# Routing and expert setup joined into one stage of a hybrid mixer, cross attention and MoE layer

## What is computed

```python
def hier_moe(xn, w_rg, b_rg, w_re, b_re, w_gate, w_up, w_down):
    glog = (xn @ w_rg + b_rg).astype(F32)
    gsel = jnp.argmax(glog, axis=-1)                  # the best of 4 groups
    pg = jnp.take_along_axis(jax.nn.softmax(glog, axis=-1), gsel[:, None], axis=-1)
    elog = (xn @ w_re + b_re).astype(F32).reshape(T, MOE_GROUPS, EXPERTS_PER_GROUP)
    elog = jnp.take_along_axis(elog, gsel[:, None, None], axis=1)[:, 0]
    top_p, top_i = lax.top_k(jax.nn.softmax(elog, axis=-1), TOP_K_INNER)
    gate = pg * top_p / jnp.sum(top_p, axis=-1, keepdims=True)
    ...
    padded = (counts + MOE_BLOCK - 1) // MOE_BLOCK * MOE_BLOCK   # blocks of 128 rows
    ...
    def expert_block(args):
        xb, e = args
        h = jax.nn.silu(xb @ w_gate[e]) * (xb @ w_up[e])
        return h @ w_down[e]
```

## Time and profile before

| | us |
|---|---|
| median of 3 runs | 2595.21 |
| these runs | 2592.27 to 2596.45 |
| the profiled execution | 2593.17 |
| its span, first to last instruction | 2591.3 |
| TensorE busy | 2309.0 (89%) |
| VectorE busy | 1400.4 (54%) |
| ScalarE busy | 981.1 (38%) |
| mean granted TensorE clock | 0.951 of full speed |

### The profile page before, as it was taken

One profiled execution on the slowest core, in us unless ns is written; L12 is line 12 of the kernel. 1 busy time (PEld: TensorE's weight loads), 2 busy tenths in 40 slices (PEclk: granted clock), 3 DMA queues, 4 the chain that ended last, 5 costly groups with the idle time before them and its releaser, 6 DMA issues. The chain is left out here.

```text
span 2591.3 us, 34611 instructions
## 1 busy us (share of the span) xinstructions
PE 2309.0 (89%) x12015; PEld 1308.7 (51%) x12016; DVE 1400.4 (54%) x2029; ACT 981.1 (38%) x1421; POOL 339.3 (13%) x277
## 2 busy tenths in 40 slices
PE   4999999999919988999999998179999999999980
PEld 2465565655618973555555554134444444444440
DVE  5566555664628843333333332757557677757823
ACT  4522533323211332222212221146446577657723
POOL 0022121220220000000000000002221222122212
PEclk8999999999959999999999999589999999999995
DMA  5201001010060133110111001369779999999927
GB/s 187 86 25 58 1 25 58 1 49 1 9 221 25 50 123 124 49 65 34 65 66 60 31 33 49 129 239 346 253 250 302 308 321 342 338 317 328 341 66 283
DMA packets 151797, 366.52 MB, mean 141 GB/s; under 512 B 24720, under 2 KB 30736, under 8 KB 151440
## 3 DMA queue, kind: packets, MB, share of 16 engines
q1 hardware_dynamic: 133120, 305.28, 32.3%
q0 software_dynamic: 13824, 50.34, 8.0%
q10 hardware_dynamic: 4752, 9.51, 1.0%
HBM read 303.75 MB, written 61.34 MB: 141 GB/s over the span
## 5 line engine op out<-in xcount | busy, mean ns | idle before, releaser
L110 PE MATMUL bankA<-wi,hnT 128*128 128x512 f16 (+1 forms) x1536 | 303.3, 356 | 5.5 <-DVE wi L498 5.5
L110 PE MATMUL bankE<-wg,xT 128*128 128x512 f16 x1152 | 262.2, 385 | 25.7 <-DVE xT L2432 21.5
L110 PE MATMUL bankE<-wu,xT 128*128 128x512 f16 x1152 | 259.0, 382 | 0.0
L110 PE MATMUL bankE<-wd,hT 128*128 128x512 f16 x1152 | 256.5, 379 | 1.7 <-DVE hT L2437 1.7
L110 PEld LDWEIGHTS bankA<-wi,hnT 128*128 128x128 f16 x1536 | 151.7, 99 | 148.8 <-issue 7.4
L110 PEld LDWEIGHTS bankE<-wg,xT 128*128 128x128 f16 x1152 | 113.9, 99 | 166.1 <-issue 34.3
L110 PEld LDWEIGHTS bankE<-wd,hT 128*128 128x128 f16 x1152 | 112.6, 98 | 137.6 <-issue 1.9
L110 PE MATMUL bankA<-hnT,wi 128*128 128x512 f16 x768 | 172.3, 387 | 9.0 <-DVE hnT L474 9.0
L110 PEld LDWEIGHTS bankE<-wu,xT 128*128 128x128 f16 x1152 | 113.3, 98 | 127.4 <-issue 3.3
L110 PE MATMUL bankC<-w_probs,probsT 128*128 128x512 f16 x768 | 172.0, 381 | 0.0
L110 PE MATMUL bankC<-score_w,hnT_c 128*128 128x512 f16 x768 | 170.7, 379 | 0.0
(11 more groups left out here) (400 smaller groups left out, 3402.1 us busy)
## 6 DMA issues: line engine op xcount, KB each, us to landing
w_rows<-in_w_gate SPq DMA_DIRECT2D x64, 1024.0 KB
w_rows<-in_w_up SPq DMA_DIRECT2D x64, 1024.0 KB
w_rows<-in_w_down SPq DMA_DIRECT2D x64, 1024.0 KB
xg<-in_x SPq DMA_DIRECT2D x4, 2048.0 KB, 10.9
cat_t<-scratch_cat SPq DMA_DIRECT2D x16, 512.0 KB, 4.9
Hc<-in_x SPq DMA_DIRECT2D x16, 512.0 KB, 5.6
scratch_ybuf<-Hc SPq DMA_DIRECT2D x16, 512.0 KB, 2.6
hf<-scratch_ybuf SPq DMA_DIRECT2D x16, 512.0 KB, 11.8
```

Source lines behind the costliest of these rows:

```text
L110: ins = pe.matmul(o, a[x][k], b[y][k], start=start and k == 0 and j == 0, stop=stop and k == n - 1 and j == 2)
```

## The change

`route` is no longer a stage of its own. Its code stands at the head of each engine's code in `experts`, in the same block. Six things differ:

- the table of constants, now `cst_all` with 784 columns, is loaded once, as the first DMA of the cross stage in the place of the identity alone (128 columns), and kept; the loads of `cst_r`, `iota_e`, `tok_e` and `cst_e` are gone;
- SP loads all six pieces of expert 0 as the first thing of the stage, without reading a plan. So that expert 0 is the first in use in any case, its number of blocks is raised to at least 1 (one more operation on `nblk`);
- VectorE makes the places (`destf`) and the row lists right behind `end`, and the block plan after `rows_to`. A new semaphore `planned` tells it; the engines wait on it before they read `plan` (SP after the first six loads, GpSimd after two gathers, the others at the loop or, for VectorE, in order);
- the gate lists (split of the gates, three multiplications, 32 products) move behind the up products of block 0 on TensorE and behind the rests of gate and up on VectorE; `gate_of` is taken after the rests of down;
- in VectorE's `first`, the rest of x of block 0 moves between the rests of gate and those of up; on ScalarE the nearest values of down come before x;
- the intermediate tiles of the routing lie in slot 1 of `wd` and in `y0` and `y1`, which are free by then, and the products in `bankE`.

The core of the diff:

```diff
-        ident, nhalf, gf = sb("cst_c", [P, P]), sb("nhalf_c", [P, 2]), sb("g_ffn", [P, D])
+        ident, nhalf, gf = cst[:, K_ID:K_ID + P], sb("nhalf_c", [P, 2]), sb("g_ffn", [P, D])
...
-            sp.dma_start(ident[:, :], dram["cst"][:, K_ID:K_ID + P]).then_inc(ld, 16)
+            sp.dma_start(cst[:, :], dram["cst"][:, 0:K_GAM]).then_inc(ld, 16)
...
-            sp.dma_start(iota[:, :], dram["cst"][:, K_IOTA:K_IOTA + P]).then_inc(ld, 16)
-            sp.dma_start(tok[:, :], dram["cst"][:, K_TOK:K_TOK + NCH]).then_inc(ld, 16)
-            sp.dma_start(ident[:, :], dram["cst"][:, K_ID:K_ID + P]).then_inc(ld, 16)
-            e0 = expert(0)
-            for p in GU:
-                load(p, e0)
-            for i in range(HB):
-                sp.wait_ge(x_ld[i], 16)
-            for p in DN:
-                load(p, e0)
+            for p in GU + DN:
+                load(p, slice(0, 1))
+            sp.wait_ge(planned, 1)
             gate_up_rows(1)
...
             LATE = 2
-            for t in range(NT + LATE):
+            gather(0)
+            gather(1)
+            pool.wait_ge(planned, 1)
+            used = turns_used(pool)
+            for t in range(1, NT + LATE):
...
         def steps(eng, first, step, last):
 
+            first()
+            eng.wait_ge(planned, 1)
             used = turns_used(eng)
-            first()
...
             def first():
-                for p in GU:
+                for p in GU + DN:
                     nearest(p, 0, 0)
                 take_x(0, 0)
-                for p in DN:
-                    nearest(p, 0, 0)
                 silu(0, 0)
...
+            do(ts, nblk[:, 0:1], nblk[:, 0:1], 1.0, None, ALU.max)
+            do(dve.tensor_tensor_scan, end[:, :], one, nblk[:, :], 0.0, ALU.mult, ALU.add)
+
+            do(tt, first_blk[:, :], end[:, :], nblk[:, :], ALU.subtract)
+            do(ts, first_row[:, :], first_blk[:, :], float(P), None, ALU.mult)
...
             dve.tensor_scalar(rows_from[:, :], row_f[:, :], float(T - 1), None, ALU.min).then_inc(rows_ok, 1)
             dve.tensor_copy(rows_to[:, :], row_f[:, :]).then_inc(rows_ok, 1)
...
+            do(ts, used_e[:, :], nblk[:, :], 0.0, None, ALU.is_gt)
+            do(dve.tensor_tensor_scan, rank[:, :], one, used_e[:, :], 0.0, ALU.mult, ALU.add)
...
+            dve.wait_ge(cnt, 2)
+            dve.tensor_copy(plan[:, 0:PL_TURNS], bank[6][0:1, 2 * NE:2 * NE + PL_TURNS]).then_inc(planned, 1)
...
             def first():
-                gate_up_rest(0, 0)
+                for p in GU[0:2]:
+                    rest(p, 0, 0)
                 x_rest(0, 0)
+                for p in GU[2:]:
+                    rest(p, 0, 0)
+                gates_listed()
                 down_rest(0, 0)
+                gates_taken()
                 product(0, 0)
...
             def first():
                 turn_x(0, 0, 0)
                 gate_up(0, 0)(0, 0)
+                gates_listed()
                 turn_x(1, 1, 0)
```

More of the change, by code:

```diff
@@ L2141, in experts @@
-def experts(nc, env, dram, gates, destf, plan):
+def experts(nc, env, dram, logits, cst):
     FT = DE // P
@@ new lines, in work @@
+        def work(k, *shape):
+            n = int(np.prod(shape))
+            v = spare[k][:, spent[k]:spent[k] + n]
+            spent[k] += n
+            letters = "abc"[:len(shape)]
+            return v.rearrange(f"p ({' '.join(letters)}) -> p {' '.join(letters)}", **dict(zip(letters, shape)))
+        oh = work(1, 2, NCH, NE)
+        e32, pos = work(2, NCH, NGR, EPG), work(2, NCH, NE)
+        both, before, cum, again = (work(0, NE, NCH) for n in range(4))
+        E8, t8, m8, O8 = (work(0, NCH, EPG) for n in range(4))
@@ new lines, in experts, with flat @@
+        G4, O4, t4 = (work(0, NCH, NGR) for n in range(3))
+        c1 = work(0, 8, NCH)
+        nblk, first_blk, end, used_e, rank, eq, t32, first_row = (work(0, NE) for n in range(8))
+        cols, turns_f = work(0, 6), work(0, 1)
+        c_expert, c_u, c_block, c_split, c_more, c_half = (cols[:, i:i + 1] for i in range(6))
+        lt, ones, one = cst[:, K_LT:K_LT + P], cst[:, K_ONE:K_ONE + P], cst[:, K_ONE:K_ONE + NE]
+        def flat(t):
+            return t[:, :, :].rearrange("p e c -> p (e c)")
@@ L2167, in experts @@
+        row_f, pad_f, gate_of = work(0, NB), work(0, NB), sb("gate_of", [P, NB])
         bank = [ctx.enter_context(nc.psum_tensor(f"bankE{i}", [P, 512], F32)) for i in range(8)]
-        ld = sem("e_consts")
+        r_steps, a_s, cnt, summed, ready, planned = (sem(n) for n in (
+            "route_steps", "route_exp", "counts_done", "pairs_summed", "again_ready", "plan_ready"))
         w_ld = [sem(f"w_rows_loaded{p}") for p in range(6)]
@@ L2368, in _ @@
         def _(dve):
-            dve.wait_ge(ld, 48)
-            ch = Chain(dve, lists)
+            ch = Chain(dve, r_steps)
+            tt, ts, stt, red = dve.tensor_tensor, dve.tensor_scalar, dve.scalar_tensor_tensor, dve.tensor_reduce
+            seen = []
+            dve.memset(again[:, :, :], 1.0).then_inc(ready, 1)
+            dve.wait_ge(ready, 1)
+            dve.memset(again[:, :, 0:1], 0.0).then_inc(ready, 1)
+            dve.wait_ge(ready, 2)
             def do(f, *a):
```

317 lines of the change are left out of this document (135 added, 182 removed).

## The result

| | before | after |
|---|---|---|
| median of 4 runs each, us | 2593.82 | 2575.45 |
| these runs | 2592.27 to 2596.45 | 2574.24 to 2577.27 |
| the profiled execution | 2593.17 | 2574.76 |
| its span | 2591.3 | 2572.9 |

What follows compares the result with a forecast made beforehand. Loop bound by TensorE, its start by a chain mostly on VectorE; gains of 11.74 us up to `rows_to` and 6.67 from there to block 1 sum to 18.4, so 2593.17 becomes 2574.8 us, range 2570 to 2583.

Steps and rivals of the forecast that it cites:

- What bounds: Loop at TensorE's pace, so the kernel's end follows block 1's start, set by a chain mostly on VectorE, 1621 to 1714 us.
- Part 1: Stage start to the end of `rows_to`: 11.74 us shorter, ending at 1655.00 instead of 1666.74.
- The table's 2.31: Stage start: with the table already loaded, VectorE's first reduction comes at 1621.36 instead of 1623.67, saving 2.31 us.
- 3.67 for the change of stage and three constants: Routing on VectorE: the 3.67 us that `blk` sat idle for `cst_e` goes.
- Part 2: From `rows_to` to block 1's gate products: 40.42 us instead of 47.09, a gain of 6.67.
- the rests of down with the gate lists beside them: Ahead of block 1: 4.48 us on VectorE beside 4.44 of lists on TensorE, 4.6 with a semaphore.
- The cover of x: Block 0: gather lands in 6.3 us, x ready at 1664.3 against gate rests ending at 1664.9, 0.6 us spare.
- Rival 1: x or the start-up costs more, together 4 to 7 us, about 2580.5 us; chance 0.14.
- The rule against it: First gather's descriptors beside the plan's short VectorE operations: if GpSimd were kept out, x 2.2 us later, kernel 2576.4.
- The plan's move: Block plan moved behind `rows_to`: 5.52 us leaves part 1 and comes back in part 2.
- The early weights: Expert 0's six pieces, issued at 1620.5, are split at about 1643, 17 us before the first rest.
- The cross stage: Its first DMA grows from 64 to 392 KB: no cost, 1 us if the 2.6 us cover failed.

Runs made afterwards that it cites:

- the last experiment: Three gate multiplications moved from VectorE to GpSimd, against the changed kernel with block 1's x taken before the second expert's up rests: 2569.2 us, 0.9902 of before.
- a third kernel: Gate lists moved back ahead of the first rests on VectorE and TensorE, against the changed kernel: 2583.26 us, 0.9955 of before.

## Why the prediction was right

**What bounds.** The loop passes on what comes ahead of it: shown by 828.7 to 834.3 us for it in all kernels, whether block 1 starts at 69 or at 95 us.

**Part 1** was to give 11.74; it gave 11.39. The table's 2.31 is exact in after, and block 1 moved by 2.56 when it was put back alone. 3.67 for the change of stage and three constants is borne out by the missing gap; it wasn't tested alone. Most of the 0.35 us missing came from a step that the sum didn't have: the count products of the routing, for which VectorE's wait ahead of `nblk` grew from 2.01 to 2.43 us. TensorE made them in 3.80 us at a granted clock of 0.58 in before and in 4.32 at 0.50 in after.

**Part 2** was to give 6.67; it took 39.90 us instead of 40.42. Each of its terms lies within 0.2 us of the rows. The largest two misses: the plan took 5.34 to the first rest instead of 5.52, and for the rests of down with the gate lists beside them I took 4.6, with the lists at 4.44; this step took 4.41. The lists were 2.81, since TensorE came to them at full clock, and lay wholly under the rests of down. The text beside the sum says that `sg` waited for 12.5 us; that is how long block 0's products took, while VectorE was idle for 8.31 of it. The sum doesn't use the figure.

**The cover of x** was given as 0.6 us and was 2.3: ScalarE was done with x at 1661.39 and VectorE came to it at 1663.66. The step that failed is the landing, taken as 6.3 from the earlier trace rows: it was 4.5. Rival 1, x late, lost its ground with that. The gather had been measured beside other work; in its new place it had none.

**The rule against it** had the sign wrong. I had set the plan's short operations beside the multiplications as the same danger. (The prediction's 1658.3 us is where the descriptors would end at 3.00 us, not the issue, which the sum has at 1655.3; a gather kept out until 1660.5 would have been 5.2 us late and not 2.2.) In after the first gather's descriptors took 1.24 and the second's 0.94 us beside the plan's short steps, against 3.00 and 1.74 beside the multiplications. With VectorE idle they took 1.24 and 0.95 too, so the short steps cost nothing that can be seen. The Trainium skill, SBUF — State Buffer, section "Who interferes with whom", says that a VectorE instruction with two SBUF inputs contends with a GpSimd instruction that reads SBUF; the last experiment agrees, with 7.91 and 10.11 us for pairs of rests of 4.47 beside GpSimd's multiplications. The same section infers of `tensor_tensor` that it doesn't hold up the building of descriptors. The runs speak against that: 3.00 us beside the `tensor_tensor` multiplications and 3.00 beside the rests, both with two SBUF inputs, 1.24 without either, and 7.87 for a gather beside four rests in a row (the kernel with x taken later), which ended 0.82 us after the last of them. Whether it is the writing of descriptors that waits, or GpSimd's reading of the row numbers, isn't told apart.

**The plan's move** I booked as −5.52 and +5.52, nothing on the chain but an earlier gather. The sum came out, but the place is worth 7.2 us: 5.4 of earlier issue and 4.6 of shorter landing, less the cover. VectorE takes x in two halves, and the second, which sets the end, had 2.9 us of cover in after: 7.1. What was missing in my account is that each step moved also decides what runs beside the others.

**The early weights.** That they were ready I had; that the new order of ScalarE rests on them I hadn't seen, and the first kernel without them showed it by 8.5 us.

**The cross stage** was to cost nothing: the cat tile is turned 9.34 us after the stage's first DMA, 9.37 before, with 328 KB more ahead of it. Its landing took 6.8 us instead of 5.9, inside the cover.

**What the parts are worth**, each undone alone, in us of block 1's start: weights early 11.1 (19.6 with ScalarE's order), gate lists later 8.7, plan behind the lists 7.2, table 2.6. They sum to 29.6, more than the 18.6 measured, so such prices don't add: each was taken from a kernel that is arranged for all the others. The early weights show it. In before the four pieces of gate and up were split by 1669.85, 10 us ahead of VectorE's first rest (1679.90); there, early weights alone had nothing to shorten. That is read from the rows; no kernel had them alone.

## What to carry to other kernels

Put short work that nobody waits for yet (here the block plan) right behind the step that starts a transfer, and the long operations behind the landing; price a transfer by what will run beside it in its new place, not by its old row. Where an engine waits at the head of a loop, list what the waiting instruction really needs, and move all else on the supplying engine behind it: a few lines of order gave a further 5.8 us here. And before work is given to an idle engine, look at what that engine shares with the one to be relieved.

## What the runs showed of the hardware

- The first indirect gather of 128 rows landed in 4.5 to 4.7 us beside short steps of VectorE or none, 6.2 beside VectorE's rests, 9.1 beside the rests and 1 MB weight loads. A gather's instruction on GpSimd took from 0.94 us to 7.87.
- A GpSimd multiplication (128x2048 f16) and VectorE's operation on two SBUF tiles took turns, instruction by instruction: the latter stood at 2.29 us when it came first and at 4.49 to 5.70 when it didn't. Moving 6.94 us across made the kernel no faster.
- The same 32 products took 4.44 us at a granted clock of 0.62, behind 8.34 us of idleness, and 2.81 at 1.00, right behind other products; behind 8.80 us of idleness in a third kernel, 5.05 at 0.54.
- The loop of 47 blocks varies by 5.6 us between executions of like kernels, while the 75 us before it repeat within 0.02.
